# End of the first mixer: order of VectorE and ScalarE work, of the mean products, and of the first output rows

## The reference

```python
y_a = sc_b * depthwise_conv(sc_c * sc_h, w_sc_conv)          # short convolution, 3 taps
o   = rms_norm(o_f + o_b, g_gla_head)                        # gated linear attention ("retention")
y_b = o * silu(gg)
y_c = blocked_attention(q_c, k_c, v_c, ...)                  # attention
y_d = silu(layer_norm(depthwise_conv(a * sigmoid(gate), w_cfm_dw), g_cfm_ln, b_cfm_ln))   # conformer
y   = concatenate([rms_norm(yb, gb) for yb, gb in zip((y_a, y_b, y_c, y_d), gains)], axis=-1)
return y @ w_out
```

## Time and profile before

| | before |
|---|---|
| median of 3 runs | 3172.69 us (3171.29 to 3172.72) |
| profiled execution: time, span from first to last instruction | 3168.69 us, 3167.0 us |
| mean granted TensorE clock | 0.953 |
| busy: PE, ACT, DVE, POOL | 2880.3, 1434.8, 1796.5, 1090.9 us |
| share of PE in the span | 91% |

### The profile page before, as it was taken

One profiled execution on the slowest core, in us unless ns is written; L12 is line 12 of the kernel. 1 busy time (PEld: TensorE's weight loads), 2 busy tenths in 40 slices (PEclk: granted clock), 3 DMA queues, 4 the chain that ended last, 5 costly groups with the idle time before them and its releaser, 6 DMA issues.

```text
span 3167.0 us, 45541 instructions
## 1 busy us (share of the span) xinstructions
PE 2880.3 (91%) x13552; PEld 2321.7 (73%) x13552; DVE 1796.5 (57%) x2649; ACT 1434.8 (45%) x2027; POOL 1090.9 (34%) x643
## 2 busy tenths in 40 slices
PE   6888999999879999999999977999499999969994
PEld 5666888876658888877877866887368777748883
DVE  4875534135674442157654157998558643269996
ACT  4525455225343554212345135887113453238884
POOL 2213344543213444635643521110356544501101
PEclk9998999999989999999999988999699999979997
DMA  4212233432113333534321347998334222449994
GB/s 123 67 34 80 80 99 94 160 104 69 47 40 94 95 97 114 179 87 107 107 70 51 104 154 269 411 411 337 116 96 117 81 61 78 159 142 410 411 411 156
DMA packets 379302, 468.87 MB, mean 148 GB/s; under 512 B 35122, under 2 KB 281988, under 8 KB 379076
## 3 DMA queue, kind: packets, MB, share of 16 engines
q1 hardware_dynamic: 353664, 392.05, 36.8%
q0 software_dynamic: 14688, 53.48, 4.4%
q10 hardware_dynamic: 10724, 20.65, 2.2%
HBM read 423.62 MB, written 35.65 MB: 145 GB/s over the span
## 4 chain that ended last, share of the span: by engine, by line
PE 47%; issue 33%; POOL 12%; DVE 4%; DMA 2%; ACT 2%; ACTq 1%; POOLq 0%; SPq 0%; DVEq 0%
POOL unit_lo L411 10%; PE bank L491 7%; PE bank L492 6%; PE bank L2041 4%; PE bank L2183 4%; PE bank L2184 4%; PE bank L2187 4%; PE bank L806 2%; PE bank L2197 2%; PE bank L2198 2%; PE bank L2201 2%; PE bank L2114 1%; PE bank L906 1%; PE bank L907 1%; PE bank L909 1%
## 5 line engine op out<-in xcount | busy, mean ns | idle before, releaser
L411 POOL TENSOR_TENSOR unit_lo<-unit_raw,unit_hi 128x1024 fp32r<-128x1024 f32 (+2 forms) x194 | 465.5, 2402 | 881.7 <-ACT unit_hi L404 881.5
L491 PE MATMUL bank<-xT_hi,unit_hi 128*128 128x512 f32 (+1 forms) x1776 | 694.2, 394 | 11.1 <-DVE d_lo L2645 3.7
L492 PE MATMUL bank<-xT_lo,unit_hi 128*128 128x512 f32 (+1 forms) x1776 | 671.7, 382 | 0.0
L491 PEld LDWEIGHTS bank<-xT_hi,unit_hi 128*128 128x128 f32 x1776 | 339.5, 191 | 99.6 <-issue 30.2
L492 PEld LDWEIGHTS bank<-xT_lo,unit_hi 128*128 128x128 f32 x1776 | 339.7, 191 | 64.9 <-issue 6.0
L404 ACT ACTIVATE unit_hi<-unit_raw 128x1024 fp32r<-128x1024 f32 (+2 forms) x194 | 203.0, 1048 | 383.9 <-PE bank L806 152.7
L396 POOL TENSOR_TENSOR unit_lo<-unit_raw,unit_hi 128x1024 fp32r<-128x1024 f32 (+3 forms) x154 | 316.8, 2057 | 12.8
L394 POOL TENSOR_SCALAR unit_hi<-unit_raw 128x1024 fp32r<-128x1024 f32 (+3 forms) x154 | 145.0, 942 | 476.3 <-PE bank L2041 267.6
L476 DVE TENSOR_TENSOR wt_lo<-wt,wt_hi 128x1024 fp32r<-128x1024 f32 x192 | 229.0, 1221 | 31.7 <-ACT wt_hi L471 30.7
L476 DVE TENSOR_TENSOR xT_lo<-wt,xT_hi 128x1024 fp32r<-128x1024 f32 x192 | 234.4, 1223 | 12.4 <-ACT xT_hi L471 2.5
L806 PE MATMUL bank<-xT_hi,unit_lo 128*128 128x512 f32 x976 | 241.2, 389 | 0.0
(11 more groups left out here) (519 smaller groups left out, 6209.3 us busy)
## 6 DMA issues: line engine op xcount, KB each, us to landing
wt<-in_w SPq DMA_DIRECT2D x384, 512.0 KB, 8.4
unit_raw<-in_w_in SPq DMA_DIRECT2D x276, 256.0 KB, 3.1
unit_raw<-in_w_ffn_up SPq DMA_DIRECT2D x176, 256.0 KB, 3.1
unit_raw<-in_w_ffn_down SPq DMA_DIRECT2D x88, 256.0 KB, 3.0
unit_raw<-in_w_out SPq DMA_DIRECT2D x64, 256.0 KB, 2.8
y_rows<-yb POOLq DMA_DIRECT2D x30, 512.0 KB, 7.6
y_rows<-zeros POOLq DMA_DIRECT2D x24, 512.0 KB, 5.2
unit_raw<-in_w_br SPq DMA_DIRECT2D x96, 128.0 KB, 2.3
```

Of the source, the lines that this page charges most:

```text
L411: pool.eng.tensor_tensor(lo, raw, hi.bitcast(F32), SUB).then_inc(self.split, 1)
L491: pe.matmul(out, wh, xh, start=first, stop=False)
L492: pe.matmul(out, wh, xl, start=False, stop=False)
```

## The change

- `short_conv` no longer waits for or multiplies by the gate. The multiplication is a function of its own, `conv_gated`. `short_conv(1)` moves into step 16 of the loop on VectorE, ahead of `gla_heads`; `conv_gated(1)` stands behind `attended(3)`.
- VectorE then runs `tok_y_v` of retention before the layer norm of the conformer, the low parts of retention before `tok_y_v` of attention, and the convolution before the conformer at the end.
- ScalarE takes retention's root first, then squares `ya`, then issues the gain and bias loads and makes the two weight parts. The mean products swap places: the third is now `ya`'s in bank 1, the fourth `u`'s in bank 0. Both logarithms run one after the other, then both exponentials.
- TensorE turns attention behind unit 0's products on tiles 2 and 3. Units 0 and 1 then run on tile 0 once both logarithms have read banks 0 and 1 (`a_step` 11), and on tile 1 once attention's low parts have been read out of banks 2 and 3.
- `OUT_ORDER` takes the convolution's rows (0, 1) before the conformer's (6, 7).

```diff
-        OUT_ORDER = (2, 3, 4, 5, 6, 7, 0, 1)
+        OUT_ORDER = (2, 3, 4, 5, 0, 1, 6, 7)
...
                 late()
+                if late_1:
+                    for k in range(SPLIT):
+                        passes(k, 0, True, True)
+                    late_1()
                 for k in range(SPLIT):
-                    for i in range(2):
+                    for i in range(1 if late_1 else 0, 2):
                         last = passes(k, i, True, True)
                     last.then_inc(ring.done, 1)
...
             rms_t(T, 4, 7, 2, 0)
-            T.eng.wait_ge(tok_lo.sem, tok_lo.at(T, 2))
-            tok_t(T, 1, og2)
...
+                elif k == 1:
+                    tok_t(T, 1, og2)
+
+            def sums_read():
+                T.eng.wait_ge(a_step.sem, a_step.at(T, 11))
+
+            def rows_read():
                 T.eng.wait_ge(tok_lo.sem, tok_lo.at(T, 4))
...
+            tok_sd_a(A, 2, 4, 1.0 / W)
+            A.eng.wait_ge(rms_in.sem, rms_in.at(A, 2))
+            squares_a(A, ya)
             load_gb(A, t["ln1_g"][bass.ds(l, 1), :], t["ln1_b"][bass.ds(l, 1), :])
             for j in range(U_OUT, U_OUT + SPLIT):
                 ring.high(A, j)
             for i in range(2):
                 A.eng.wait_ge(cfm_ln.sem, cfm_ln.at(A, i + 1))
                 act.activation(u[:, i, :], u[:, i, :], ACT.Silu, bias=col(B_CF + i)).then_inc(a_step.sem, a_step.up(A))
+            tok_hi_a(A, 0, 2)
             A.eng.wait_ge(a_step.sem, a_step.last(A))
+            A.eng.wait_ge(rms_mm.sem, rms_mm.at(A, 4))
             squares_a(A, [u[:, i, :] for i in range(2)])
-            tok_sd_a(A, 2, 4, 1.0 / W)
             tok_sd_a(A, 3, 4, 1.0 / W)
-            rstd_a(A, 3, 1)
-            tok_hi_a(A, 0, 2)
-            A.eng.wait_ge(rms_in.sem, rms_in.at(A, 2))
-            A.eng.wait_ge(rms_mm.sem, rms_mm.at(A, 4))
-            squares_a(A, ya)
-            rstd_a(A, 4, 0)
+            for r, b in ((3, 1), (4, 0)):
+                A.eng.wait_ge(rms_mm.sem, rms_mm.at(A, r + 1))
+                act.activation(rstd[:, r % 2, :], bank[b][:], ACT.Ln, bias=eps).then_inc(a_step.sem, a_step.up(A))
+            A.eng.wait_ge(a_step.sem, a_step.last(A))
+            for r in (3, 4):
+                act.activation(rstd[:, r % 2, :], rstd[:, r % 2, :], ACT.Exp, scale=-0.5).then_inc(rms_rs.sem, rms_rs.up(A))
+            gain_a(A, 0, 0, ya)
             tok_hi_a(A, 1, 4)
-            gain_a(A, 0, 6, [u[:, i, :] for i in range(2)])
-            gain_a(A, 2, 0, ya)
+            gain_a(A, 2, 6, [u[:, i, :] for i in range(2)])
...
+                if n == 16:
+                    short_conv(1)
                 if n == 17:
                     gla_heads()
             attended(3)
+            conv_gated(1)
+            tok_y_v(V, 2, og)
             V.eng.wait_ge(rms_rs.sem, rms_rs.at(V, 3))
             for i in range(2):
                 v.scalar_tensor_tensor(u[:, i, :], u[:, i, :], col(G_CF + i), rstd[:, 0, :], MUL, MUL).then_inc(cfm_ln.sem, cfm_ln.up(V))
                 V.eng.wait_ge(cfm_ln.sem, cfm_ln.last(V))
-            tok_y_v(V, 2, og)
             V.eng.wait_ge(m_or.sem, m_or.last(V))
             tok_ms_v(V, W, og2)
-            short_conv(1)
+            tok_lo_v(V, 0, 2)
             tok_y_v(V, 3, og2)
-            tok_lo_v(V, 0, 2)
```

More of the change, by code:

```diff
@@ L894, in splits1, with rows_products @@
                     G.eng.dma_start(y_dram[rows, :].rearrange("p (x c) -> p x c", c=P), over(zeros[:].unsqueeze(1), [P, KC, P])).then_inc(y_zero.sem, y_zero.up(G))
-        def rows_products(T, tile, first, count, held, x_hi, x_lo, late=None, order=None, ready=None):
+        def rows_products(T, tile, first, count, held, x_hi, x_lo, late=None, late_1=None, order=None, ready=None):
             def passes(k, i, hi, lo):
@@ L1159, in rows_ready @@
                     T.eng.wait_ge(g_oev.sem, g_oev.at(T, 8))
-            def banks_free():
-                T.eng.wait_ge(rms_rs.sem, rms_rs.at(T, 5))
+                elif k == 1:
[3 more added lines that the diff above has]
+            def rows_read():
                 T.eng.wait_ge(tok_lo.sem, tok_lo.at(T, 4))
-            rows_products(T, 0, U_OUT, KC, len(OUT_HOMES) // 2, *([x[:, k, :] for k in range(KC)] for x in (xT_hi, xT_lo)), late=banks_free, order=OUT_ORDER, ready=rows_ready)
+            rows_products(T, 0, U_OUT, KC, len(OUT_HOMES) // 2, *([x[:, k, :] for k in range(KC)] for x in (xT_hi, xT_lo)), late=sums_read, late_1=rows_read, order=OUT_ORDER, ready=rows_ready)
             begun_units(T, 0, U_UP)
@@ L1417, in short_conv @@
             def short_conv(i):
-                c, hh, b = (proj[:, SLOT[x + i], :] for x in (6, 8, 4))
-                V.eng.wait_ge(proj_ev.sem, proj_ev.at(V, POS[4 + i] + 1))
+                c, hh = (proj[:, SLOT[x + i], :] for x in (6, 8))
+                V.eng.wait_ge(proj_ev.sem, proj_ev.at(V, max(POS[6 + i], POS[8 + i]) + 1))
                 v.tensor_tensor(scp[:, i, 1:S + 1], c, hh, MUL).then_inc(v_step.sem, v_step.up(V))
@@ L1427, in short_conv, with conv_gated @@
                     V.eng.wait_ge(v_step.sem, v_step.last(V))
+            def conv_gated(i):
+                V.eng.wait_ge(proj_ev.sem, proj_ev.at(V, POS[4 + i] + 1))
                 raised = rms_in if i else v_step
-                v.tensor_tensor(ya[i], ya[i], b, MUL).then_inc(raised.sem, raised.up(V))
+                v.tensor_tensor(ya[i], ya[i], proj[:, SLOT[4 + i], :], MUL).then_inc(raised.sem, raised.up(V))
                 V.eng.wait_ge(raised.sem, raised.last(V))
@@ L1588, in vector1 @@
                     short_conv(0)
+                    conv_gated(0)
                 if n == 14:
@@ L1603, in vector1 @@
                 V.eng.wait_ge(cfm_ln.sem, cfm_ln.last(V))
-            tok_y_v(V, 2, og)
             V.eng.wait_ge(m_or.sem, m_or.last(V))
             tok_ms_v(V, W, og2)
-            short_conv(1)
+            tok_lo_v(V, 0, 2)
             tok_y_v(V, 3, og2)
-            tok_lo_v(V, 0, 2)
             V.eng.wait_ge(rms_rs.sem, rms_rs.at(V, 4))
             for i in range(2):
-                v.tensor_tensor(u[:, i, :], u[:, i, :], rstd[:, 1, :], MUL).then_inc(y_val.sem, y_val.up(V))
+                v.tensor_tensor(ya[i], ya[i], rstd[:, 1, :], MUL).then_inc(y_val.sem, y_val.up(V))
                 V.eng.wait_ge(y_val.sem, y_val.last(V))
-            tok_lo_v(V, 1, 4)
             V.eng.wait_ge(rms_rs.sem, rms_rs.at(V, 5))
             for i in range(2):
-                v.tensor_tensor(ya[i], ya[i], rstd[:, 0, :], MUL).then_inc(y_val.sem, y_val.up(V))
+                v.tensor_tensor(u[:, i, :], u[:, i, :], rstd[:, 0, :], MUL).then_inc(y_val.sem, y_val.up(V))
                 V.eng.wait_ge(y_val.sem, y_val.last(V))
-            gain_v(V, 0, 6, [u[:, i, :] for i in range(2)])
-            gain_v(V, 2, 0, ya)
+            gain_v(V, 0, 0, ya)
+            tok_lo_v(V, 1, 4)
+            gain_v(V, 2, 6, [u[:, i, :] for i in range(2)])
             norm_v(V, 0, U_OUT + KC - 1)
```

## The result

| | before | changed |
|---|---|---|
| median of 6 runs each | 3171.29 us (3169.18 to 3172.72) | 3155.34 us (3148.98 to 3158.52) |
| ratio | | 0.9948 (0.9938 to 0.9958) |
| profiled execution, span | 3167.0 us | 3154.5 us |

The changed kernel is faster, by 0.52%. The forecast was 3154.7 us. A second set of runs of the same changed kernel gave 3149.85 us against 3171.07 us, a ratio of 0.9935 (0.9918 to 0.9951).

What follows compares the result with a forecast made beforehand. The mixer's end was taken as bound by the chain VectorE, ScalarE, TensorE, then from 280 us TensorE alone. Layer gains 9.3 + 8.7 = 18.0 us took the median from 3172.7 to 3154.7 us; range 3146 to 3162.

Steps and rivals of the forecast that it cites:

- The convolution in the wait: Four convolution instructions moved into VectorE's 3.56 us idle time: cost nothing, 0.3 us to spare; uncovered, up to 2.8 us.
- Retention's root first: ScalarE's root at 256.4 instead of 262.77, so VectorE's division ends at 257.9 and retention's turn comes 6.4 us earlier.
- VectorE held up by GpSimd: GpSimd's 5.1 us shift onto VectorE's square of attention, adding 2.2 us; sums end at 264.1, covered by 2.4 us.
- held up twice: Lower bound on the cover of VectorE's attention sums before ScalarE wants them: 0 us.
- The clock at the start of the products: TensorE at the lower clock: mean product of `u` 3.78 us, and 0.9 us extra on the first output matmuls.
- `rows_read`: TensorE's wait for attention's low parts: read by 277.0, TensorE arrives at 278.5, covered by 1.5 us.
- Pairing: ScalarE's logarithms together, then exponentials: four table loads become two, worth about 1 us for each layer.
- The ring: Weight parts behind the output start: unit 2 wait 0 to 0.2 us, GpSimd's cover about 0.9 us; 0.1 us taken.
- Layer 1: Same stretch 667.15 us later: gain 8.2 us, plus 0.5 us taken for a luckier clock rise.
- What follows the stretch moves up as a whole: Work after each stretch is TensorE's own and was claimed to move earlier by the full gain.
- The rival on the clock elsewhere: Later work meets other clock steps: 0.04 for a loss over the bound, 0.03 for eating two thirds of the gain.
- The signs of being wrong: TensorE idle behind the 36th output matmul, `u`'s mean product after 267, or later span parts changing over 3 us.

Runs made afterwards that it cites:

- the swap: Changed kernel with attention's high and low parts ahead of the convolution's on ScalarE and VectorE; 3152.29 us, ratio 0.9933.
- the attempt with the early weight part: Changed kernel with the first output weight part before ScalarE's last eviction and attention's high and low parts ahead of the convolution's; 3148.62 and 3148.24 us.

## Why the prediction was right, point by point

The time and the size were right: 18.0 us forecast, 15.95 measured in the first set and 21.2 in the second. The path was right too: the chain through VectorE, ScalarE and TensorE was what could be shortened, and M became shorter by 10.95 and 9.85 us where 9.3 and 8.7 were forecast. That the total of the first set came so close owes something to luck: the stretches gave 2.8 us more than forecast, and in the profile of that set 8.3 us were lost outside them. Times "on the forecast's scale" below are those of the changed kernel less 5.63 us, by which its reduction started later.

- **The convolution in the wait.** Forecast: free, and 2.8 us if uncovered. Shown from both sides: 2.8 us by taking it back, nothing by doing it alone.
- **Retention's root first.** Forecast 6.4 us for the turn of retention. From the start of the reduction to the end of the division it was 264.30 - 253.71 = 10.6 us and became 263.55 - 259.34 = 4.2 us, 6.4 us less. On the forecast's scale the root ran at 256.08 and the division at 256.69, where 256.1 and 256.7 were written down. The part as a whole is worth 4.7 us.
- **VectorE held up by GpSimd: a term that was mis-sized.** I took one loss of 2.2 us, on the square of attention, and wrote that retention's low parts would be done at 265.6. There were two losses of 2.0 us, on the conformer (3.52 against 1.54 us alone, where I took 1.4) and on the square. ScalarE waited only 0.2 us for the sums, but the low parts stand behind both in VectorE's list and came at 273.18 - 5.63 = 267.55. The bound for "held up twice" was set against ScalarE's root alone and not against what is queued behind it. At the forecast's start of the products, 268.5, they would still have been in time. TensorE waited 1.62 us for them only because the mean product was done early, and the whole wait is worth 0.5 us (M 42.16 without it).
- **The clock at the start of the products: mis-sized the other way.** The forecast put the lower level there because TensorE would stand still ahead of the conformer's squares, from about 262 to 264.7. It stood still for 0.72 us only. I took 3.78 us for the mean product and 0.9 us more for the first products. Both ran at the upper level, 1.98 us and nothing. Together with the wait the first product came at 273.31 - 5.63 = 267.7, 0.8 us sooner than forecast, and the 49th at 279.7 where 281.3 was forecast. The clock gave 2.7 us and the late low parts took about 1 us of it back.
- **`rows_read`.** A cover of 1.5 us was forecast. The low parts of attention end at 282.25 and the 37th matmul starts at 282.54, with no gap, so 0.3 us of cover were left. The low parts were 0.4 us sooner than forecast, but TensorE was there 1.6 us sooner. Pairing, forecast at about 1 us, is what keeps this cover (1.8 us measured).
- **The ring.** Forecast wait at unit 2: 0 to 0.2 us. The matmul at 285.30 starts 0.27 us behind the one ahead of it, where 0.23 is usual.
- **Layer 1.** I had given it 8.2 us plus half of 1 us of luck. It gained 9.85 us: the clock was again at the upper level ahead of the products.
- **What follows the stretch moves up as a whole.** Nearly. The layer norm of layer 0 starts 5.3 us earlier than before, the reduction of layer 1 4.0 us, the layer norm of layer 1 13.8 us, and the last instruction 12.5 us. So 1.4 us were lost between the stretches and 1.3 us behind them, within the 3 us that the prediction allowed. The head, which is all that stands ahead of the first stretch, lost 5.6 us. The rival on the clock elsewhere was priced from a difference of 1.1 us between the layers; in this profile all that was lost outside the stretches came to 8.3 us. In the profile of the second set the head lost 2.5 us and the span was 18.7 us shorter.
- **The signs of being wrong.** TensorE did not stand still behind the 36th matmul. The mean product of `u` started at 269.70, which is past 267, but at 264.07 on the forecast's scale. The sign was written as a time from the start of the span, and so it also caught the loss of the head.

**What stays open.** Nothing ahead of the reduction of layer 0 differs between the kernels, except the convolution in the last steps, which the kernel with the convolution alone has too. Yet the reduction started at 253.6 to 253.7 us in the three profiles with the old order at the end of the mixer, and at 254.1 to 260.8 us in the eleven with the new order or a variant of it. The profiles part more than 200 us ahead of the changed code, in TensorE's clock. The stretch from 30 to 40 us, before:

```profile
30.00:40.00 10.00, 5.71 (x35) 5.06 (x34) 9.12 (x14) 2.35 (x5) 0.00 (x0) 0.62 0.05 16
```

The same stretch of the changed kernel:

```profile
30.00:40.00 10.00, 5.71 (x26) 5.08 (x25) 9.12 (x14) 2.35 (x5) 0.00 (x0) 0.50 0.05 16
```

| granted clock from 30 to 40 us | profiles | start of the reduction, layer 0 |
|---|---|---|
| 0.62 to 0.63 | 3, the old order | 253.6 to 253.7 |
| 0.59 to 0.60 | 2 | 254.1 and 255.6 |
| 0.56 to 0.57 | 4 | 256.2 to 256.3 |
| 0.50 | 5 | 258.9 to 260.8 |

From group to group, the less of these 10 us ran at the upper level, the later the stretch starts. A second difference follows from 148 to 153 us: the clock is at 1.00 in the first two groups and at 0.66 to 0.70 in the other nine profiles. So what goes with the start of the stretch is TensorE's clock from its first rise on. That no instruction of the change has a part in it is likely and not shown. Why the kernels with the old order met the same clock three times isn't known, and three profiles may be chance. M leaves the head out. But M of the kernel before was measured at this one place of the clock only, while 42.7 was found in three profiles at different ones (starts of 256.2, 259.3 and 260.5 us, the last with the swap). The two layers before differ by 1.1 us, so my estimate is that the 20.8 us are uncertain by about as much.

## What to carry to other kernels

Where an engine's list is reordered, follow every held-up instruction to what stands behind it in that engine's list, not only to its own reader. A part that gains nothing alone can be worth its full length once the list it feeds is led by its reader: here 0 and 2.8 us. When TensorE waits in several short pieces, try useful work between them. Here the clock stayed up with it, and that was about half of the gain of turning attention behind the first unit.

## What the runs showed of the hardware

VectorE instructions with two inputs in SBUF and GpSimd's subtractions held each other up. With GpSimd's two subtractions of 2.4 us beside them, two VectorE groups took 3.52 and 3.25 us; without, 1.54 and 1.23. GpSimd's pair in turn took 5.17 us in place of 4.76. The square of attention (1.23 us alone) started at 267.14 and ended 1.08 us after GpSimd's pair was over at 269.31, so it did nearly all of its work behind it. The Trainium skill (SBUF — State Buffer, section "Who interferes with whom") says that VectorE instructions with two SBUF inputs contend with a GpSimd instruction that reads SBUF, and the runs agree. The reduction, with one input, was not lengthened: in the attempt with the early weight part it ran wholly beside a subtraction of GpSimd and took 1.22 us.

```profile
254.07 1.22 DVE L1400 TENSOR_REDUCE gst<-glu 128x4 f32<-128x1024 f32 x1
```

GpSimd in the same place:

```profile
253.76 2.50 POOL L411 TENSOR_TENSOR unit_lo<-unit_raw,unit_hi 128x1024 fp32r<-128x1024 f32 x1 [20.79 <-ACT unit_hi L404]
```

One kernel's layer 0 took 43.55 us in one execution and 41.10 in another (M), with the granted clock at 0.50 in the first and at 1.00 in the second over the first products. A load of ScalarE's tables took 1.28 us and stood ahead of each change between logarithm and exponential.
